# State space layer of a two-block transformer kernel: the chunk recurrence by turned inputs and a scan instruction

## The reference

```
a_bar = exp(lam * dt)
b_bar = ((a_bar - 1.0) / lam)[..., None] * complex(b_re, b_im)
bu = einsum('blgh,gph->blgp', u, b_bar)
_, states = associative_scan(_ssm_combine, (a_seq, bu), axis=1)   # x[l] = a_bar * x[l-1] + bu[l]
y = einsum('blgp,ghp->blgh', states, c).real + d_skip * u
```

## Time and profile before

| | |
|---|---|
| median of 3 runs | 3087.39 us |
| the profiled execution | 3085.57 us, its span 3083.7 us |
| TensorE busy | 2835.6 us, 92% |
| VectorE busy | 1865.7 us, 61% |
| ScalarE busy | 1415.3 us, 46% |
| GpSimd busy | 295.4 us, 10% |

### The profile page before, as it was taken

How to read it: one execution, slowest core, us unless ns; L and a number is a source line. 1 busy time by engine, 2 the same in 40 slices (tenths; PEclk the granted TensorE clock), 3 DMA queues, 4 the chain that set the end, 5 groups by cost and what they waited for, 6 DMA issues and landing times.

```text
span 3083.7 us, 35863 instructions
## 1 busy us (share of the span) xinstructions
PE 2835.6 (92%) x12864; PEld 2221.4 (72%) x12864; DVE 1865.7 (61%) x2163; ACT 1415.3 (46%) x1806; POOL 295.4 (10%) x288
## 2 busy tenths in 40 slices
PE   7999999995999999999997469999989999899998
PEld 1547888874777777777775347888876767788887
DVE  3435654454889989998888684544323784454432
ACT  2323323323777777777775514333223347433321
POOL 1200100051001001010011000000011221000000
PEclk8999989995999999999998779999999999999999
DMA  6920732313898999999996622222221110022221
GB/s 232 337 88 31 282 111 84 124 67 150 330 374 349 380 361 361 370 354 379 354 367 240 50 74 80 89 101 99 96 91 69 54 57 28 28 96 96 96 96 69
DMA packets 90802, 546.93 MB, mean 177 GB/s; under 512 B 9232, under 2 KB 18848, under 8 KB 32384
## 3 DMA queue, kind: packets, MB, share of 16 engines
q1 hardware_dynamic: 79584, 485.65, 42.7%
q0 software_dynamic: 10816, 59.58, 5.5%
q10 hardware_dynamic: 288, 0.15, 0.0%
HBM read 516.51 MB, written 41.42 MB: 181 GB/s over the span
## 4 chain that ended last, share of the span: by engine, by line
PE 74%; DVE 14%; issue 6%; ACT 4%; DMA 2%; POOL 1%; DVEq 0%; ACTq 0%; SPq 0%; POOLq 0%
PE bank L400 41%; PE bank L338 6%; PE bank L1286 5%; PE bank L1289 5%; PE bank L1290 5%; DVE expert_low L2347 3%; DMA arena<-in_we_stream 1%; ACT expert_high L1746 1%; PE bank L1270 1%; PE bank L1537 1%; DVE expert_x_low L2432 1%; DVE arena L2476 1%; PE bank L1545 1%; PE bank L1471 1%; DVE arena L2563 1%
## 5 line engine op out<-in xcount | busy, mean ns | idle before, releaser
L2347 DVE TENSOR_TENSOR expert_low<-arena,expert_high 128x2048 fp32r<-128x2048 f32 x291 | 690.3, 2403 | 90.1 <-ACT expert_high L1746 72.4
L1746 ACT ACTIVATE expert_high<-arena 128x1024 fp32r<-128x1024 f32 x582 | 598.7, 1058 | 204.4 <-PE bank L1286 118.3
L803 DVE TENSOR_TENSOR weight_parts<-ring_pages,weight_parts 128x1024 fp32r<-128x1024 f32 x185 | 227.5, 1230 | 459.0 <-ACT weight_parts L795 458.0
L795 ACT ACTIVATE weight_parts<-ring_pages 128x1024 fp32r<-128x1024 f32 x185 | 195.9, 1060 | 449.1 <-PE bank L400 406.5
L400 PE MATMUL bank<-high_b,weight_parts 128*128 128x512 f32 x1168 | 373.1, 401 | 13.1 <-DVE low_p L2585 7.6
L400 PE MATMUL bank<-low_b,weight_parts 128*128 128x512 f32 x1056 | 353.9, 389 | 0.0
L1286 PE MATMUL bank<-expert_high,expert_x_low 128*128 128x512 f32 x768 | 305.5, 398 | 23.5 <-DVE expert_low L2347 21.9
L1289 PE MATMUL bank<-expert_high,expert_x_high 128*128 128x512 f32 x768 | 300.4, 391 | 0.0
L1290 PE MATMUL bank<-expert_low,expert_x_high 128*128 128x512 f32 x768 | 300.4, 391 | 0.0
L400 PEld LDWEIGHTS bank<-high_b,weight_parts 128*128 128x128 f32 x1168 | 219.4, 190 | 76.0 <-issue 25.0
L400 PEld LDWEIGHTS bank<-low_b,weight_parts 128*128 128x128 f32 x1056 | 198.2, 188 | 41.4 <-issue 0.5
(11 more groups left out here) (479 smaller groups left out, 4432.2 us busy)
## 6 DMA issues: line engine op xcount, KB each, us to landing
arena<-in_we_stream SPq DMA_DIRECT2D x294, 1024.0 KB, 6.7
ring_pages<-in_wb_stream SPq DMA_DIRECT2D x93, 1024.0 KB, 4.8
ring_pages<-in_wa_stream SPq DMA_DIRECT2D x49, 1024.0 KB, 4.8
arena<-in_mod POOLq DMA_DIRECT2D x16, 1024.0 KB
xbuf<-arena POOLq DMA_DIRECT2D x25, 512.0 KB, 15.9
arena<-xbuf SPq DMA_DIRECT2D x17, 512.0 KB, 7.4
ybuf<-arena SPq DMA_DIRECT2D x16, 512.0 KB, 2.6
arena<-kd SPq DMA_DIRECT2D x8, 512.0 KB, 22.5
```

Of the source, the lines that this page charges most:

```text
L795: nc.scalar.activation(high, src, ACT.Copy).then_inc(weights_high, 1)
L803: nc.vector.tensor_tensor(low, src, high.bitcast(F32), ALU.subtract).then_inc(weights_split, 1)
L1746: nc.scalar.activation(ehigh[c % HIGH_E][:, at], ring_e[c % RING_E][:, at], ACT.Copy) \
L2347: nc.vector.tensor_tensor(elow[c % RING_E][:], ring_e[c % RING_E], ehigh[c % HIGH_E][:].bitcast(F32), ALU.subtract).then_inc(weights_split ...
```

## The change

- The factor of a chunk is split into its size (`size8`) and a pure turn (`c8`, `s8`, with one correction step that brings its length to 1). The squarings move from before the expert loop to behind the zeros of `kd` (in the last expert block).
- GpSimd, after its last store of `kd`, fills `shrink` (the size, repeated, with a zero at the start of each group's 16) and builds `turn_table`, the turns by 1 to 16 chunks for every group, by doubling: sixteen instructions. ScalarE and VectorE wait for it before the chunk inputs.
- The chunk inputs go to `zs`, in four segments of 16 chunks. VectorE turns them back in place: `zs * cos - turned * sin`, with the quarter turn still made by TensorE. A complex recurrence becomes a real one.
- For each segment VectorE adds the carry, runs `tensor_tensor_scan` twice (32 groups each) and turns the results forward into `xs`; the quarter turn of the scanned values is a new TensorE product, `zj`. The residual's turns and the `yu` products are placed between these.
- `mt` is loaded in two halves of the groups. The first half no longer waits for the inputs to be turned. The halves of `mt` change places in memory; `ytm` moves to free pages, and one tile of copied `yu` goes to `zs`.
- The output is stored tile by tile, each after its own sum.

```
-            sp.wait_ge(bank_done, JB[f"ux{2 * KT - 1}"] + 1)
...
+            for part in range(2):
+                if part:
+                    sp.wait_ge(S["gains_in"], 16 * 5)
+                    sp.wait_ge(bank_done, JB[f"ux{2 * KT - 1}"] + 1)
+                for s in range(S5T):
+                    lo = (S5T - s) * S5H
+                    sp.dma_start(mflat[16 * s:16 * s + 16, half_g * (1 - part):half_g * (2 - part)],
+                                 kflat[:, half_g * part:half_g * (part + 1), lo:lo + P]) \
+                        .then_inc(S["gains_in"] if part else mt_in, 16)
...
-            sp.wait_ge(S["b_x_ready"], 4 * KT)
-            sp.dma_start(out.rearrange("k p t -> p k t"), x).then_inc(S["b_stored"], 16)
+            for j in range(KT):
+                sp.wait_ge(S["b_x_ready"], 3 * KT + j + 1)
+                sp.dma_start(out[j], x[:, j, :]).then_inc(S["b_stored"], 16)
...
+            ta, tb = scaled[:, 0, :], scaled[:, 1, :]
+            for _ in range(3):
+                link(nc.gpsimd.tensor_tensor(ta, c8, c8, ALU.mult))
+                link(nc.gpsimd.tensor_tensor(tb, s8, s8, ALU.mult))
+                link(nc.gpsimd.tensor_tensor(s8, s8, c8, ALU.mult))
+                link(nc.gpsimd.tensor_tensor(s8, s8, s8, ALU.add))
+                link(nc.gpsimd.tensor_tensor(c8, ta, tb, ALU.subtract))
+                link(nc.gpsimd.tensor_tensor(size8, size8, size8, ALU.mult))
...
+            coef = shrink.rearrange("p (g j) -> p g j", j=SEG)
+            link(nc.gpsimd.memset(coef[:, :, 0:1], 0.0))
+            link(nc.gpsimd.tensor_copy(coef[:, :, 1:SEG], size8.unsqueeze(2).to_broadcast([P, S5G, SEG - 1])))
+            for i in range(2):
+                pool.wait_ge(k_stored[i], 16 * (KT // 2 + (i == 0)))
+            link(nc.gpsimd.tensor_copy(turn_table[:, :, :, 0], ab8[:, :, 0, :]))
+            n = 1
+            while n < SEG:
+                src, dst, other = turn_table[:, :, :, 0:n], turn_table[:, :, :, n:2 * n], turned_part[:, :, :, 0:n]
+                by = [turn_table[:, i, :, n - 1:n].unsqueeze(1).to_broadcast([P, 2, S5G, n]) for i in range(2)]
+                link(nc.gpsimd.tensor_tensor(other, src, by[1], ALU.mult))
+                link(nc.gpsimd.tensor_tensor(dst, src, by[0], ALU.mult))
+                link(nc.gpsimd.tensor_tensor(dst[:, 0], dst[:, 0], other[:, 1], ALU.subtract))
+                link(nc.gpsimd.tensor_tensor(dst[:, 1], dst[:, 1], other[:, 0], ALU.add))
+                n *= 2
+            pool.sem_inc(S["b_coef_ready"], 1)
...
+            for k in range(NSEG):
+                for h in range(2):
+                    pe.wait_ge(S["b_scanned"], 2 * k + h + 1)
+                    ps = opened(f"zj{k}{h}")
+                    pe.matmul(ps[:], quarter, zs[:, k, half_at * h:half_at * (h + 1)], start=True, stop=True) \
+                        .then_inc(bank_done, 1)
+                if k < 2:
...
+                    continue
+                pe.wait_ge(mt_in, 16 * S5T)
...
+            pe.wait_ge(S["gains_in"], 16 * (5 + S5T))
             held = {}
...
-            pe.wait_ge(S["b_scanned"], 1)
+            pe.wait_ge(S["b_scanned"], 2 * NSEG + 1)
...
             for m in range(KT):
...
+                part(nc.vector.tensor_tensor(side, ps, sin, ALU.mult))
+                part(nc.vector.tensor_tensor(z, z, cos, ALU.mult))
                 dve.wait_ge(dve_step, steps[0])
+                dve.sem_inc(free(f"sj{m}"), 1)
+                link(nc.vector.tensor_tensor(z, z, side, ALU.subtract))
+            carry = scaled[:, 0, :]
+            for k in range(NSEG):
+                z = zs[:, k, :]
+                by_group = z.rearrange("p (g j) -> p g j", j=SEG)
+                if k:
+                    link(nc.vector.tensor_tensor(carry, xs[:, :, SEG * k], size8, ALU.mult))
+                    link(nc.vector.tensor_tensor(by_group[:, :, 0], by_group[:, :, 0], carry, ALU.add))
+                halves = [slice(half_at * h, half_at * (h + 1)) for h in range(2)]
+                for at in halves:
+                    nc.vector.tensor_tensor_scan(z[:, at], shrink[:, at], z[:, at], 0.0, ALU.mult, ALU.add)                         .then_inc(S["b_scanned"], 1)
+                dve.wait_ge(S["b_scanned"], 2 * k + 2)
+                states = xs[:, :, SEG * k + 1:SEG * k + SEG + 1]
+                link(nc.vector.tensor_tensor(states, by_group, turn_table[:, 0], ALU.mult))
+                for h, at in enumerate(halves):
+                    link(nc.vector.tensor_tensor(z[:, at], result(dve, f"zj{k}{h}")[:], flat_table[:, 1, at], ALU.mult))
+                    dve.sem_inc(free(f"zj{k}{h}"), 1)
+                link(nc.vector.tensor_tensor(states, states, by_group, ALU.add))
```

More of the change, by code:

```diff
@@ L130 @@
     JOBS_B += ([f"s{_m}"] if _m < KT else []) + ([f"sj{_m - 1}"] if _m else [])
-JOBS_B += [f"xf{j}" for j in range(KT)] + [f"yu{b}" for b in range(KT)] + [f"ys{b}" for b in range(KT, 2 * KT)]
+SEG = 16
+NSEG = S5C // SEG
+BESIDE = [[f"xf{j}" for j in range(4)], [f"xf{j}" for j in range(4, KT)], [f"yu{b}" for b in range(4)],
+          [f"yu{b}" for b in range(4, KT)]]
+for _k in range(NSEG):
+    JOBS_B += [f"zj{_k}0", f"zj{_k}1"] + BESIDE[_k]
+JOBS_B += [f"ys{b}" for b in range(KT, 2 * KT)]
 LAST_FIRST = (4, 5, 6, 7, 0, 1, 2, 3)
@@ L524, in block_kernel @@
         decay = sb("decay", [P, 2, 48])
-        wgate = sb("wgate", [64, 2, 4 * P])
+        wgate = sb("wgate", [P, 2, 4 * P])
         stats = sb("stats", [P, 2, 6])
@@ L685, in block_kernel @@
         u2 = page(16, S5G, S5C)
-        xs = page(29, S5C + 1, 2, S5G)
+        xs = page(29, S5G, S5C + 1)
+        zs = page(33.0625, S5C // SEG, S5G * SEG)
         cp = page(20, S5G, S5T + 1, S5H)
@@ L701, in block_kernel, with mt_tile, inputs_part @@
         tmpc = page(45.625, 4 * (S5T + 1) * S5H)
-        scaled = page(47.75, 2, 2, S5G)
-        ytm = [page(41.25 + i, S5T, P) for i in range(2)]
+        scaled = page(47.75, 2, S5G)
+        ytm = [page(37.25 + i, S5T, P) for i in range(2)]
+        turn_table = page(45.625, 2, S5G, SEG)
+        turned_part = page(35, 2, S5G, SEG // 2)
+        sine_part = page(48.5, 512)
+        shrink = wgate.rearrange("p a b -> p (a b)")
+        block_at, half_at = S5G * SEG // KT, S5G * SEG // 2
+        def mt_tile(kt):
+            return (kt + KT // 2) % KT
+        def inputs_part(kt):
+            return mt[0:S5C, mt_tile(kt)] if kt != 3 else zs[0:S5C, 0, :].rearrange("p (g n) -> p g n", n=P)
         tstat = page(48, 8, NTX)
@@ L963, in _ @@
             pool.wait_ge(S["b_coef_exp"], 3)
+            link(nc.gpsimd.tensor_copy(c8, are))
+            link(nc.gpsimd.tensor_copy(s8, aim))
+            link(nc.gpsimd.tensor_copy(size8, size))
             link(nc.gpsimd.tensor_tensor(sin4, sin4, size.unsqueeze(1).to_broadcast([P, 4, S5G]), ALU.mult))
@@ L977, in _ @@
                 link(nc.gpsimd.tensor_tensor(pw[:, k + 1, :, :], pw[:, k + 1, :, :], t2, ALU.add))
[L979 to L987, removed]
-            link(nc.gpsimd.tensor_scalar(ab8[:, 1, 1, :], i8, -1.0, None, ALU.mult))
             pool.wait_ge(S["b_s5_in"], 80)
@@ L1380, in _ @@
                     ps = opened(f"sj{m - 1}")
-                    pe.matmul(ps.rearrange("p (c g) -> p c g", g=8), quarter, xs[:, 1:S5C + 1, 0, 8 * m - 8:8 * m],
-                              start=True, stop=True).then_inc(bank_done, 1)
+                    pe.matmul(ps.rearrange("p (k n) -> p k n", k=NSEG), quarter,
+                              zs[:, :, block_at * (m - 1):block_at * m], start=True, stop=True).then_inc(bank_done, 1)
             pe.wait_ge(S["tile_made"], 3 * NTX)
-            for j in range(KT):
-                ps = opened(f"xf{j}")
-                for t in range(NTX):
-                    ins = pe.transpose(ps[:, t * P:(t + 1) * P], x1t[:, t, j * P:(j + 1) * P], ident[:])
-                ins.then_inc(bank_done, 1)
@@ L1390, in from_inputs @@
             def from_inputs(o, g, start, stop):
[L1391 removed]
+                return pe.matmul(o[0:S5C], u2[:, g, :], mt[:, mt_tile(g // 8), g % 8, :], start=start, stop=stop)
             def from_states(o, g, start, stop):
[L1394 removed]
+                return pe.matmul(o[0:S5C], xs[:, g, 0:S5C], cp[:, g, 1:S5T + 1, :].rearrange("p k h -> p (k h)"),
@@ L2556, in _ @@
[L2556 to L2563 removed]
+                at = slice(block_at * m, block_at * (m + 1))
```

61 lines of the change are left out of this document (33 added, 28 removed).

## The result

The median of six runs with the change is 3067.11 us (3054.87 to 3077.8), beside 3087.18 us (3079.82 to 3094.38) of six runs without it on the same chip: ratio 0.993, 95% interval 0.9907 to 0.9953. The prediction said 3068.9. The profiled execution took 3067.94 us.

What follows compares the result with a forecast made beforehand. Nearly all of the chain is TensorE's matmuls, left alone. 23.4 + 1.9 + 5.2 + 0.5 - 0.5 = 30.5, less 12.0, is 18.5 us: 3085.57 becomes 3067.1 profiled, median 3068.9, range 3056 to 3080.

Steps and rivals of the forecast that it cites:

- The scan: VectorE between expert loop and GLU: four segments, eight scans at 1.23 us, 28.7 us in all against 73.2.
- TensorE's queue is late next: Behind the last turned segment, TensorE's in-order products set the end; the states start 23.4 us earlier.
- The held banks: TensorE's eight `ys` banks behind the fourth segment: 2.03 us a bank, 16.2 us.
- clock term: TensorE cold before `yu4` and warm at the states: 1.2 us lost, 1.9 us won.
- The table: GpSimd's turn table beside VectorE's token-row instructions, each shutting the other out: 12.0 us lost on the chain.
- The walk: Stepping through GpSimd's and VectorE's lists while token rows form: 12.0 us lost of 18.8 us of GpSimd work.
- The load: Toeplitz matrix from DRAM in halves, landing about 1721 and 1757: TensorE's wait goes, but no separate gain.
- the 21.8 us wait: TensorE's idle time for the Toeplitz load in the kernel before, claimed to go.
- The store: Output at the kernel's end, eight stores instead of one of 2 MB: 5.2 us saved.
- The squarings: GpSimd's three squarings leave the early part (664 to 673): 0.5 us gained, within -2 to +2.
- The last expert block: 22 small GpSimd instructions run there beside VectorE's L2347: 0 to 2 us lost, 0.5 taken.
- The sum: Whole kernel: gains and small losses of 30.5 us, less 12.0, give 18.5 us saved.

Runs made afterwards that it cites:

- the repeat: The changed kernel, unedited, timed and profiled once more: 3069.78 us, ratio 0.9937.
- the version to keep: Changed kernel with the last two table doublings after the token rows, TensorE's products reordered and no zero products: 3040.42 us, ratio 0.9856.

## Why the prediction was right, point by point

The time came out right partly by luck: its parts were right in mechanism but for one, and the errors in size cancelled.

- **The scan.** Taken at 1.23 us, measured 1.21; predicted 28.7 us from its start to its end, measured 28.7 (1759.6 to 1788.3). Right, with small errors that cancel: the first segment took 7.2 us instead of 6.8, for it waited 0.8 for TensorE, the others 7.2 instead of 7.3. The Trainium skill ("DVE: opcode table, instruction layouts, handler registers and perf-mode slots", section "Datapath and trigger behaviour") calls it half throughput; the traces come near, 1.21 beside 0.69 us for a product of the same shape, 1.76 times.
- **TensorE's queue is late next.** Right: no idle behind the fourth segment in any trace, and the two kernels that shorten this queue, the products moved and the zero products taken out, gain 8.6 and 11.7 us in this stage against the repeat. Up to the held banks the prediction was 1.7 us too slow (64.4 us behind the first `ux`, measured 62.8), because the clock was warmer than taken: 8.76 us for the 64 records of `ux` instead of 9.68, 3.71 for the last 32 of `yu` instead of 4.5, and the 1.2 us that the sum added for a cold `yu` did not come either.
- **The held banks.** This is the step that failed. Priced at 16.2 us, because the earlier trace rows show them at 2.03 us, they took 25.5. The sum had a clock term for `yu` and for the states (1.2 lost, 1.9 won; the states' part and what follows won 1.5), and took it as given that a busy engine stays at 2.4 GHz. The trace of the kernel before spoke against this: the last eight records of its held banks took 1.91 us instead of 1.09, with no gap before them. Worth 9.3 us in the profiled execution, 2.4 in the repeat.
- **The table.** Right in mechanism (VectorE and GpSimd shut each other out on the chain) and in sign, mis-sized: 12.0 predicted, 7.2 measured. The walk let a GpSimd instruction block VectorE for its full duration. The rows show a loss of 0.8 to 0.9 us by a 128x512 and 1.7 by a 128x1024, which take 1.15 and 2.0 alone, and 0.1 to 0.4 in a VectorE instruction that lies beside small ones, of 64 to 256 elements. By these differences about 0.2 to 0.3 us of each doesn't shut VectorE out, an estimate, and for a small one that is a large part of it. The Trainium skill's rule ("SBUF — State Buffer", section "SBUF: two separate sides") of a lock held for the whole instruction is too dear by that here; what GpSimd does in the rest of its instruction no trace shows.
- **The load.** Right that it is no gain of its own. But the prediction let the 21.8 us wait go because the first half starts early; in the kernel that loads after the turns the wait is gone as well, because the segments now stand in front of the products that need it.
- **The store.** 5.2 predicted, 5.3 measured both ways.
- **The squarings.** 0.5 predicted within -2 to +2, measured 4.6 in this trace, outside that range, and 1.8 to 4.7 in the others. The prediction named the alternative itself, that the instruction hits a weight split, and took it to be nearly as dear as the stall of 3 us; less of it arrives.
- **The last expert block.** 0.5 predicted, 2.8 here, 0.0 to 1.9 in the other traces. GpSimd's small instructions take 2.2 us beside line 2408 instead of 0.3, seven times, but that is GpSimd's wait: line 2408's 19 instructions there take 45.5 us together, 45.1 before. What made the rest of the 2.8 is open.
- **The sum.** By stages: scan and queue 25.3 predicted, 18.5 measured; table -12.0, -7.2; store 5.2, 5.3; early part 0.5, 4.6; last block -0.5, -2.8. Together 18.5 predicted, 18.4 measured; the rest of the 17.6 us is -3.6 behind the GLU and +2.7 in stretches that the change doesn't touch. So the total agreed because the clock's 9.3 us, which the sum did not hold, were outweighed by a table 4.8 us cheaper and an early part 4.1 us better. That is luck: the time was right with its two largest terms off by 7 and 5 us in opposite directions.

Open is what makes the clock fall in one execution in the third bank and in another in the seventh, where the 6 us of spread behind the GLU come from, and why the medians of several edits fall by more than their stages; none of these was tried.

## What to carry to other kernels

When a long dependent chain is replaced, price the other engine's queue behind the last hand-over and shorten that, before you shorten the new instruction: here the scan's rate was worth 1 to 2 us, perhaps 3, and the order of TensorE's products 8.6 against the repeat. Once the queue is gone, as in the version to keep, look at the instruction again. Don't use one-row products to open banks in a stretch that ends on TensorE; the first real product can open them. Work given to an idle GpSimd beside a VectorE chain of two-operand instructions costs the chain most of each large instruction (1.7 of 2.0 us) and less of the small ones (6.5 us for the sixteen here), so put the large pieces where VectorE is waiting.

## What the runs showed of the hardware

- A fully busy TensorE fell to a granted clock of 0.50 (1.2 GHz) in every trace with a zero product of one row (1*64, 1x512) in each held bank, seven traces with the kernel before, in the second bank at the earliest and the last at the latest, and in none of six where the same product had 128 rows or was left out. A bank then took 3.8 us instead of 2.0.
- With the 128-row zero product a held bank is also shorter at full clock: repeats come every 1.73 us instead of 2.01.
- VectorE's scan takes 1.21 us for 128x512 fp32, 1.76 times a product (0.69); GpSimd's strided doublings take 1.15 us for 128x512, no more than its contiguous 1.26 us rows.
